# One decoder layer on one core: a fourth place for the experts' w2 in two halves, expert outputs written over the gathered rows, and each gather issued after the scatter from the same buffer has landed

## The reference

```python
def hier_moe(h, rg_w, rg_b, re_w, re_b, w1, w3, w2):
    ...                                # group softmax, best group, two best of its 8 experts
    gates = ...                        # a token's weights over all 4 * 8 = 32 experts
    out = jnp.zeros((t.shape[0], d), F32)
    for gi in range(N_GROUPS):
        a = jnp.einsum("td,edf->tef", t, w1[gi]).astype(F32)
        u = jnp.einsum("td,edf->tef", t, w3[gi]).astype(F32)
        hid = jax.nn.silu(a) * u * gates[:, gi, :, None]
        out = out + jnp.einsum("tef,efd->td", hid, w2[gi].astype(F32))
    return out
```

## Time and profile before

| | before |
|---|---|
| median of 3 runs | 611.18 us (610.94 to 611.47) |
| the profiled execution's own time | 611.13 us |
| its span (first to last instruction) | 609.3 us |
| PE busy | 579.6 us (95%) |
| DVE, ACT, POOL busy | 258.1, 202.9, 183.5 us |
| mean granted PE clock, as a share of full speed | 0.997 |
| moved by DMA | 152.73 MB, 251 GB/s on average |

### The profile page before, as it was taken

How to read it: one execution, slowest core, us unless ns; L and a number is a source line. 1 busy time by engine, 2 the same in 40 slices (tenths; PEclk the granted TensorE clock), 3 DMA queues, 4 the chain that set the end, 5 groups by cost and what they waited for, 6 DMA issues and landing times.

```text
span 609.3 us, 12028 instructions
## 1 busy us (share of the span) xinstructions
PE 579.6 (95%) x4931; PEld 445.9 (73%) x4931; DVE 258.1 (42%) x598; ACT 202.9 (33%) x437; POOL 183.5 (30%) x126
## 2 busy tenths in 40 slices
PE   8999999999999999999999999999999999987894
PEld 6978887899999888857779998665566665644541
DVE  6698533781216621286632155333232332321116
ACT  6656354622333262544635222112111121111113
POOL 3444343353458421532554301111112111120011
PEclk9999999999999999999999999999999999999998
DMA  8866444222121112003798788999999999999986
GB/s 335 341 188 204 145 131 122 85 71 72 42 66 36 48 59 71 1 2 139 292 317 349 274 312 294 377 423 426 422 428 425 420 428 427 421 425 426 417 324 239
DMA packets 32087, 152.73 MB, mean 251 GB/s; under 512 B 8759, under 2 KB 12511, under 8 KB 25376
## 3 DMA queue, kind: packets, MB, share of 16 engines
q1 hardware_dynamic: 27360, 143.77, 61.2%
q0 software_dynamic: 4528, 8.15, 3.6%
q10 hardware_dynamic: 144, 0.03, 0.0%
HBM read 143.78 MB, written 16.27 MB: 263 GB/s over the span
## 4 chain that ended last, share of the span: by engine, by line
PE 65%; DMA 19%; DVE 9%; issue 4%; ACT 2%; POOL 1%; POOLq 0%; SPq 0%; DVEq 0%; ACTq 0%
PE bank L794 28%; PE bank L841 9%; DMA xg<-h2d,tok 8%; DMA w<-in_expert_w_dram 8%; PE bank L1228 5%; PE bank L1187 4%; PE bank L1202 3%; PE bank L819 2%; PE bank L1126 2%; PE bank L1140 1%; DMA yd<-oy,dst 1%; DVE Dm L1885 1%; PE bank L1120 1%; PE bank L1096 1%; DMA xt<-in_turned_dram 1%
## 5 line engine op out<-in xcount | busy, mean ns | idle before, releaser
L1569 POOL TENSOR_TENSOR wlo<-raw,whi 128x1024 fp32r<-128x1024 f32 (+1 forms) x24 | 59.1, 2466 | 84.2 <-ACT whi L1257 84.2
L1694 POOL DMA_INDIRECT yd<-oy,dst x15 | 15.1, 1009 | 163.3 <-DVE oy L2220 163.3
L1187 PE MATMUL bank<-w,xT 128*64 128x256 f32 x512 | 58.2, 380 | 3.6 <-issue 3.6
L1202 PE MATMUL bank<-w,xT 128*64 128x256 f32 x512 | 58.2, 380 | 3.4 <-DMA w<-in_expert_w_dram 3.4
L1228 PE MATMUL bank<-w,hidT 128*64 128x512 f32 x256 | 58.5, 598 | 1.7 <-ACT hidT L1546 1.7
L1187 PEld LDWEIGHTS bank<-w,xT 128*64 128x64 f32 x512 | 37.3, 137 | 27.6 <-issue 12.1
L794 PE MATMUL bank<-wlo,hHi 128*128 128x256 f32 (+2 forms) x192 | 55.9, 291 | 0.0
L1202 PEld LDWEIGHTS bank<-w,xT 128*64 128x64 f32 x512 | 36.4, 137 | 22.7 <-DMA w<-in_expert_w_dram 4.8
L794 PE MATMUL bank<-whi,hHi 128*128 128x256 f32 (+1 forms) x176 | 50.8, 288 | 1.4 <-DVE cacc L1785 1.4
L2198 DVE SCALAR_TENSOR_TENSOR hid<-bank,slot,sa 128x256 f32<-128x256 f32 x16 | 10.8, 676 | 95.2 <-issue 92.7
L794 PE MATMUL bank<-whi,hLo 128*128 128x256 f32 (+1 forms) x176 | 49.6, 282 | 0.0
(11 more groups left out here) (387 smaller groups left out, 1189.0 us busy)
## 6 DMA issues: line engine op xcount, KB each, us to landing
w<-in_expert_w_dram SPq DMA_DIRECT2D x43, 2048.0 KB, 22.3
raw<-in_w_in_dram SPq DMA_DIRECT2D x24, 512.0 KB, 3.8
w<-in_expert_w_dram SPq DMA_DIRECT2D x10, 1024.0 KB, 8.0
yd<-zt SPq DMA_DIRECT2D x8, 512.0 KB, 5.1
yt<-yd SPq DMA_DIRECT2D x4, 1024.0 KB, 9.1
raw<-in_w_in_dram SPq DMA_DIRECT2D x6, 520.0 KB, 5.9
xt<-in_turned_dram SPq DMA_DIRECT2D x4, 512.0 KB, 7.1
X<-in_x_dram SPq DMA_DIRECT2D x4, 512.0 KB, 10.7
```

What stands on the lines that cost most here:

```text
L1187: m = pe.matmul(pb[3][r, 0:FF], xT[:, c, r], w1[u % 4][:, e, c * FF:(c + 1) * FF], start=(c == 0), stop=(c == KC - 1), skip_group_check=True)
L1202: m = pe.matmul(pb[7][r, 0:FF], xT[:, c, r], w3[u % 4][:, e, c * FF:(c + 1) * FF], start=(c == 0), stop=(c == KC - 1), skip_group_check=True)
L1569: pool.tensor_tensor(low_of(g), raw_of(g), high_of(g).bitcast(F32), ALU.subtract).then_inc(wlo_done, 1)
L1694: pool.indirect_dma_start(yd.ap()[:, :], bass.IndirectOffsetOnAxis(ap=dst_i[o][:, 0:1].bitcast(U32), axis=0), oy[o][:, :], None, bounds_ch ...
```

## The change

- **A fourth place for w2.** It has two halves: w2_30 of 8 KB per partition where oy[0] and oy[1] were (and before these raw_late1 and raw_late2), and w2_31 of 8 KB at R3 + 28 KB, where sa, hid and hidT were, which move elsewhere. Units 3, 7, 11 and 15 use it and are loaded as two transfers of 1 MiB.
- **Loads.** The first half of w2 of unit 3 is issued once all granules' low parts are computed (wlo_done), the second after the third index product (idx_full) and the router's end (route_done). In the loop SP issues w2 of u + 4 in place of u + 3 after unit u, behind w1 and w3, and the loop has one turn fewer.
- **No oy.** DVE writes the combined rows over the gathered ones in xg[u % 3]. The scatter reads that buffer.
- **A wait on POOL.** Since the gather of unit u + 3 writes the buffer that the scatter of unit u reads, POOL waits ahead of the gather until that scatter has landed (scattered[u % 2]). Nothing is issued between the two.
- Small arrays that are used across the stage (rank, npi, ssf, rf) get places of their own; the two short DMAs that first raise the scatters' semaphores write to a small buffer, woken.

```diff
-        w2 = [at(f"w2_{i}", [P, 2, 2 * D], W2_AT[i]) for i in range(3)]
+        w2whole = [at(f"w2_{i}", [P, 4 * D], o) for i, o in enumerate(W2_AT)]
+        w2 = [[a[:, 2 * D * n:2 * D * (n + 1)] for n in range(2)] for a in w2whole]
+        w2.append([at("w2_30", [P, 2 * D], oy0), at("w2_31", [P, 2 * D], R3 + 28 * KB)])
-        oy = [at(f"oy{i}", [P, D], oy0 + 4 * i * KB) for i in range(2)]
...
             def load_w2(u):
-                if u == PAIRS - 1:
+                if u % 4 == 3:
...
                 if n == NOUT - 1:
+                    sp.wait_ge(wlo_done, GR)
+                    sp.dma_start(w2[3][0][:, :], ew2[3][:, 0:2 * D]).then_inc(w2_half, 16)
...
+            sp.wait_ge(idx_full, 3)
             sp.wait_ge(route_done, 1)
+            sp.dma_start(w2[3][1][:, :], ew2[3][:, 2 * D:]).then_inc(w2_full[3], 16)
...
-                for u in range(PAIRS - 3):
+                for u in range(PAIRS - 4):
...
                     sp.wait_ge(slots_freed, U + 4)
-                    load_w2(u + 3)
-                    if 4 <= u < PAIRS - 4:
+                    if u < 4:
+                        load_w2(u + 4)
+                    else:
                         load_w1(u + 4)
...
+                        load_w2(u + 4)
...
-            def scatter(U, o):
+            def scatter(U, o, s):
...
-                                        oy[o][:, :], None, bounds_check=2 * S - 1, oob_is_err=False).then_inc(scattered[o], 16)
+                                        xg[s][:, :], None, bounds_check=2 * S - 1, oob_is_err=False).then_inc(scattered[o], 16)
             def unit(p, u):
                 U, s = p * PAIRS + u, u % 3
                 if u < PAIRS - 1:
-                    scatter(U, u % 2)
+                    scatter(U, u % 2, s)
                 if u + 3 < PAIRS:
+                    pool.wait_ge(scattered[u % 2], (p * 8 + u // 2) * 16 + 32)
                     gather(U + 3, s)
...
-                    dve.scalar_tensor_tensor(out=oy[o][:, cs], in0=xg[s][:, cs], scalar=slot[:, u, 2:3], in1=pb[5 + i][:, :],
+                    dve.scalar_tensor_tensor(out=xg[s][:, cs], in0=xg[s][:, cs], scalar=slot[:, u, 2:3], in1=pb[5 + i][:, :],
                                              op0=ALU.mult, op1=ALU.add).then_inc(done, 1)
```

More of the change, by code:

```diff
@@ L485, in build @@
         fnr = at("fnr", [KC, P], 177 * KB)
+        assert oy0 + 2 * lsz <= za0 and za0 + 1792 <= W3_AT[3]
         rw = at("rw", [P, KC, NG + NE], R3 + 40 * KB)
@@ L490, in build @@
         w3 = [at(f"w3_{i}", [P, 2, KC * FF], W3_AT[i]) for i in range(4)]
[L491 removed]
+        w2whole = [at(f"w2_{i}", [P, 4 * D], o) for i, o in enumerate(W2_AT)]
+        w2 = [[a[:, 2 * D * n:2 * D * (n + 1)] for n in range(2)] for a in w2whole]
+        w2.append([at("w2_30", [P, 2 * D], oy0), at("w2_31", [P, 2 * D], R3 + 28 * KB)])
         xT = at("xT", [P, KC, P], 173 * KB)
         xg = [at(f"xg{i}", [P, D], R3 + (16 + 4 * i) * KB) for i in range(3)]
[L494 removed]
         assert oy0 + 8 * KB <= W3_AT[3] <= C0 + CONST["dm"][0] * 4 + 8 * KB and C0 + CONST["dm"][0] * 4 <= W3_AT[3]
[L496 to L498 removed]
+        sa = at("sa", [P, FF], R3 + 39 * KB)
+        hid = at("hid", [P, 2, P], R3 + 40 * KB)
+        hidT = at("hidT", [P, 2, P], za0)
+        rank = at("rank", [P, T, NE], za0 + KB)[:, :, :]
+        npi = at("npi", [P, 1], za0 + 1536, I32)
+        ssf, rf = (at(n, [P, T], za0 + 1568 + 32 * i) for i, n in enumerate(("ssf", "rf")))
+        woken = [at(f"woken{i}", [P, KC], za0 + 1632 + 32 * i) for i in range(2)]
         sel = at("sel", [P, T, 2, CAP], R3 + 36 * KB)
@@ L516, in build @@
         rv4 = lambda a, n, w: (rtA if n == 0 else rtB)[:, a:a + T * w].rearrange("p (t n) -> p t n", t=T)
-        Wt, rank, oh1, oh2, LG = rv4(0, 0, NE), rv4(128, 0, NE), rv4(256, 0, NE), rv4(384, 0, NE), rv4(512, 0, NG + NE)
+        Wt, oh1, oh2, LG = rv4(0, 0, NE), rv4(256, 0, NE), rv4(384, 0, NE), rv4(512, 0, NG + NE)
         r1 = lambda i: rtA[:, 656 + 4 * i:660 + 4 * i]
-        gm, gmx, gsum, gp, _, _, mm1, e2, den, gate0, gate1, ss2, r2, ssf, rf = (r1(i) for i in range(15))
+        gm, gmx, gsum, gp, _, _, mm1, e2, den, gate0, gate1, ss2, r2 = (r1(i) for i in range(13))
         ssp = rtA[:, 740:756]
@@ L541, in build @@
         w3_full = [sem(f"w3_full{i}") for i in range(4)]
-        w2_full = [sem(f"w2_full{i}") for i in range(3)]
+        w2_full = [sem(f"w2_full{i}") for i in range(4)]
         sel_ready = sem("sel_ready"); idx_full = sem("idx_full"); idx_ready = sem("idx_ready"); gathered = [sem(f"gathered{i}") for i in range(3)]
@@ L545, in build @@
         hid_ready = sem("hid_ready"); ht_full = sem("ht_full"); ht_ready = sem("ht_ready")
-        oyA = sem("oyA"); oyB = sem("oyB"); scattered = [sem(f"scattered{i}") for i in range(2)]; s_fn = sem("s_fn")
+        oyA = sem("oyA"); oyB = sem("oyB"); scattered = [sem(f"scattered{i}") for i in range(2)]
         s_y = [sem(f"s_y{t}") for t in range(T)]
@@ L741, in _ @@
                         load_w3(u)
-                    for u in range(3):
+                    for u in range(4):
                         load_w2(u)
@@ L1223, in unit @@
                         m.then_inc(down_half, 1)
-                        pe.wait_ge(w2_full[s], third(p, u) * 16 + 16)
+                    if u % 4 == 3 and n:
+                        pe.wait_ge(w2_full[3], (p * 4 + u // 4) * 16 + 16)
                     for c in range(2):
@@ L1239, in _ @@
                         pe.wait_ge(acc_done, 1)
-                    m = pe.matmul(pb[b][:, :], selT[:, t * P:(t + 1) * P], oy[1][:, i * 512:(i + 1) * 512], start=True, stop=t < 2)
+                    m = pe.matmul(pb[b][:, :], selT[:, t * P:(t + 1) * P], xg[(PAIRS - 1) % 3][:, i * 512:(i + 1) * 512], start=True, stop=t < 2)
                 if t < 2:
@@ L1709, in start @@
                 else:
-                    scatter(p * PAIRS - 1, 1)
+                    scatter(p * PAIRS - 1, 1, (PAIRS - 1) % 3)
                     for k in range(2):
+                        pool.wait_ge(scattered[(k + 1) % 2], p * 128 + 16)
                         gather(p * PAIRS + k, k)
```

22 lines of the change are left out of this document (11 added, 11 removed).

## The result

The changed kernel takes **655.0 us** (median of 4 runs, 653.8 to 656.4) beside 611.1 us of the kernel before (4 runs, 610.4 to 611.5): a ratio of 1.072, with an interval of 1.070 to 1.073. It is slower by 44 us, where 31 were predicted, and 2 us outside the range. The profiled execution took 654.1 us over a span of 652.3.

A forecast was written before the change was run, and what follows sets the result against it. PE bound the kernel (busy 95%), with weights at 16.0 us per unit late. At 16.1 per unit, unit 12 ends at 582.3, unit 14 at 607.5, unit 15 at 622.6; plus 17.7, span 640.3; plus 1.8, 642 us, range 622 to 653.

The forecast's parts named there:

- Which term decides: Expert stage, POOL's queue: the gather waits for the scatter's landing and pays the whole 10.3 us, not 5.8, plus 0.9.
- the 4.9 us of the fourth place: w2 of unit 3 loaded early: full stretch loses 4.9 us of PE's late weight waits, but this vanishes in the slowdown.
- In-place writes at 0: DVE's combine writing over the gathered rows: 0, bounds -0.3 to +0.3 us per unit.
- The durations: Indirect transfers under load in the expert stage: scatter 10.4 us, gather 10.3, POOL's wake-up 0.9.
- That a scatter is held behind a gather: POOL's queue: a scatter behind a gather with 9 us to go lands 5.8 us after it; no row showed this.
- loop B: One-unit loop through POOL's queue: gather 10.3, scatter held 5.8, wake-up 0.9, 17.0 us per unit; at weights' pace, chance 0.58.
- SP's queue runs dry for a moment in each unit: Expert stage: an indirect transfer then needs 4.2 us, not 10.3, so the pace settles near the weights', 16.1 per unit.
- loop A: Two-unit loop from down product through unheld scatter, wake-up, gather and turn to next but one down product: 29.9 us, 14.95 per unit.
- The signs: Expected in trace: PE waits 3 to 4 us for xg nearly every unit, scatters about 15, down products 16 to 17 apart.
- loop A alone: Rival: scatters not held behind gathers, stay at 10 to 11 us; down products alternate 17.3 and 12.6; 629.5 us, chance 0.24.
- Nothing gives way: Rival: the one-unit queue loop at 17.0 us in full, unit 12 ending at 591.3; time 651 us, chance 0.08.
- The faster case: Rival: gather costs only its turn, landing 5.8 us after POOL's wake-up; 4.9 us of weights won; 606.2 us, chance 0.07.

The follow-up runs named there:

- experiment 1: Kernel before with only POOL's wait for the scatter's landing ahead of the next gather added: 656.8 us, ratio 1.075.
- experiment 2: Changed kernel with 24 to 52 small matmuls on PE ahead of the turns behind units 2, 4, ... 12: 660.2 us, ratio 1.078.
- experiment 9: Changed kernel without w1 loads from unit 4 on, plus 24 to 60 small matmuls ahead of PE's waiting turns: 632.1 us, ratio 1.035.
- experiment 8: Changed kernel without the loads of w1 from unit 4 on, a third of the weights less: 645.1 us (one run).

## Why the prediction was right in direction and wrong in size

- **Which term decides: right.** The wait between scatter and gather is the whole loss (experiment 1), and the 4.9 us of the fourth place vanish behind it. In-place writes at 0: nothing in experiment 1 speaks against it (656.8 without, 655.0 with them and the fourth place).
- **The durations: right.** Scatter 10.4 against 10.9 and 11.7, lone gather 10.3 against 10.5, wake-up 0.9 against 522.18 - 521.3 = 0.9.
- **That a scatter is held behind a gather: right**, a step that no row of before showed. 14.9 us measured beside the predicted 9 + 5.8 = 14.8.
- **The step that failed** is the path. The prediction took loop B ("Gather 10.3, scatter 5.8, wake-up 0.9: 17.0 us per unit") as the limiting loop, and then lowered it to 16.1: "SP's queue runs dry for a moment in each unit, and in it an indirect transfer needs 4.2 and not 10.3". The queue does run dry and a gather does need 3.7 to 5.1 us then (4.7 at 522.18), but it is the second gather of each pair, for which nobody waits. That dry moment takes loop B off the chain, since the next scatter starts with no gather ahead, and gives nothing to loop A, which is what the chain that ended last runs through. From unit 2 to unit 12 the down products end at 425.0 and 593.7: 168.7 us instead of 161, 7.7 of the 12.0 us that the span is over. Only the pair from unit 2 to unit 4 was faster (31.7 us), by the gather beside the halved w2 of unit 7, for which the prediction had said that the turns come sooner.
- **The signs show it too.** Forecast were waits of 3 to 4 us in nearly every unit, scatters in about 15 and down products 16 to 17 us apart. Measured were waits in every second unit, every second scatter held, and down products 12.6 and 21.6 us apart. That alternation is the sign given for loop A alone, only longer.
- **A term that was missing: the clock.** It stands nowhere in the prediction, so it was put at nothing. After PE's waits of 2.9 to 6.1 us the turn and the down product run at 1.2 GHz (granted clock 0.50) and take 8.8 to 10.2 us for 5.7. In unit 2 the turn starts at 414.8, sooner than the predicted 415.6, and the down product ends at 425.0 instead of 421.3, 3.7 us later. After that it makes loop A 2.5 + 10.9 + 0.9 + 10.5 + 0.1 + 9.3 = 34.2 us for two units instead of 29.9: 3.6 us of it are the clock, 0.7 the two transfers. That this equals two rounds of loop B (34.0) is chance. Filling PE's even waits won nothing in the changed kernel, because loop B then came onto the chain and new slow stretches appeared in other units (experiment 2); where no scatter is held it won 13.1 us (experiment 9).
- **The rest.** From unit 12 to unit 15 39.7 us for 40.3, and the tail 18.9 for 17.7. Together 7.7 + 3.7 - 0.6 + 1.2 = 12.0 = 652.3 - 640.3.
- **The fourth place: about right, once it is visible.** The whole change is worth 5.4 us with 4 KB rows and 3.5 with 8 KB, beside the 4.9 predicted for it; with 8 KB rows 7.1 us of waits for gathers are still in it.
- **The rivals.** "Nothing gives way" (651, given 0.08) came nearest in the number, and partly by luck: its path, every scatter behind a gather, is not what ran. Loop A alone (629.5, given 0.24) had the path of the chain right. It too left out the clock, which makes 3.6 us per pair and 3.7 in unit 2 and so most of the 25.5 us that it was short, and its sign that scatters stay at 10 to 11 us failed (14.9). The faster case fell with the first gather. The estimate of 3.2 us from the Trainium skill's formula ("DMA: Bandwidth & Descriptors", "Anatomy of one DMA — SWDGE (gpsimd) path") stands beside 10.5 us measured with 16 KB rows, and 7.3 with 4 KB rows on the other queue; only idle moments come near it (3.2 to 3.7 us). The rule of the Trainium skill on the same page, "DMA: Bandwidth & Descriptors", that each DMA engine takes turns between queues packet by packet ("Queues, rings and completion order") fits the runs, as the latency falls when the other queue's packets get shorter. The trace shows no turns one by one, and the fall is smaller than in proportion.

## What to carry to other kernels

Before a wait is put between two transfers of one queue, price the second at its whole latency under the traffic of that moment and not at what it adds behind the first; then close every loop that runs through the wait, over one unit and over two, and count what the compute engine loses in clock after a wait of several us. A relief that "the queue runs dry for a moment" counts only if that moment is placed on a transfer of the limiting chain. Here the same event released the weights and, 2.5 us later, the scatter, so the gap fell on a gather that nobody waited for. A number that comes out near can stand on the wrong path: compare the pattern (which units wait, which transfers are held) as well. Where latency of a small transfer is the limit beside a stream of long rows, shorter rows of the stream are a cheap knob; of the three lengths tried 8 KB was the best.

## What the runs showed of the hardware

- A transfer of 128 rows of 4 KB (rows of empty places skipped) by the software queue, with none ahead of it and under a saturated hardware queue, lands in some 10.5 us beside rows of 16 KB, 8.5 beside 8 KB and 7.3 beside 4 KB; in a light or idle moment in 3.2 to 4.2. The stream moves 424, 419 and 409 GB/s with these rows.
- The hold in the software queue works both ways: a scatter 1.3 us behind a gather takes 14.9 us and lands 5.7 us after it.
- After a wait of PE of 2.9 to 6.1 us the turn in the changed kernel takes 1.69 to 1.97 us for 1.09 and the down product 5.0 to 6.4 for 3.65, at the 1.2 GHz level (granted clock 0.50); 20 us of PE's busy time in the whole kernel.
- The mean share of the DMA engines does not tell what a transfer meets: at 0.76 over the stage (experiment 8) scatters still took 10.7 us in the median, as the share while scatter 6 was under way was 0.91, and the gather that met a share of 0.23 took 3.6.
